# Top-k of a 384-wide score tile by the 128 scores to leave out, with 12 rounds of the 640-wide tile moved ahead of attention

## What is computed

```python
logits = einsum('bthd,bsd->bths', q_idx, k_idx) * IDX_DIM ** -0.5
score = einsum('bth,bths->bts', w_idx, relu(logits))      # w_idx = wi * N_IDX_HEADS ** -0.5
score = where(causal, score, -inf)
_, sel = top_k(score, 256)                                # per query
s = einsum('btkgd,btnkd->btkgn', q, k[sel]) * HEAD_DIM ** -0.5
o = einsum('btkgn,btnkd->btkgd', softmax(s over allowed sel), v[sel])
```

## Time and profile before

| what | value |
|---|---|
| median of 3 runs | 2638.51 us (2636.39 to 2642.58) |
| span of the profiled execution | 2639.8 us |
| mean granted clock of TensorE | 0.963 |
| PE busy over the span | 2413.0 us (91%) |
| DVE busy | 1858.0 us (70%) |
| ACT busy | 1091.3 us (41%) |
| POOL busy | 718.2 us (27%) |

### The profile page before, as it was taken

How to read it: one execution, slowest core, us unless ns; L and a number is a source line. 1 busy time by engine, 2 the same in 40 slices (tenths; PEclk the granted TensorE clock), 3 DMA queues, 4 the chain that set the end, 5 groups by cost and what they waited for, 6 DMA issues and landing times. The chain is left out here.

```text
span 2639.8 us, 35126 instructions
## 1 busy us (share of the span) xinstructions
PE 2413.0 (91%) x13848; PEld 1922.7 (73%) x13848; DVE 1858.0 (70%) x2503; ACT 1091.3 (41%) x1656; POOL 718.2 (27%) x737
## 2 busy tenths in 40 slices
PE   3988968879999999999999899787799999999998
PEld 3966824557777888787877677677687878888887
DVE  6358988984597688887755783676426688777775
ACT  5145379753343334444433442334224334444333
POOL 1332277506545201111223223323263320000000
PEclk8999979989999999999999999899899999999999
DMA  6200154224222643555441110000231344555442
GB/s 230 73 17 24 34 162 113 81 65 152 72 84 92 246 142 123 176 175 176 139 128 41 32 40 17 2 2 2 104 95 41 127 164 171 186 179 177 162 149 80
DMA packets 173849, 282.19 MB, mean 107 GB/s; under 512 B 13407, under 2 KB 86900, under 8 KB 173686
## 3 DMA queue, kind: packets, MB, share of 16 engines
q1 hardware_dynamic: 159184, 255.38, 29.7%
q10 hardware_dynamic: 14502, 24.58, 2.6%
HBM read 252.52 MB, written 27.33 MB: 106 GB/s over the span
## 5 line engine op out<-in xcount | busy, mean ns | idle before, releaser
L1448 ACT ACTIVATE w_hi<-raw 128x1024 fp32r<-128x1024 f32 x198 | 209.0, 1057 | 369.4 <-DVE raw L2123 163.7
L2106 DVE TENSOR_TENSOR w_lo<-raw,w_hi 128x1024 fp32r<-128x1024 f32 x198 | 255.5, 1291 | 126.5 <-ACT w_hi L1448 126.2
L2890 PE MATMUL ps<-w_hi,us_hi 128*128 128x512 f32 x784 | 310.2, 396 | 17.2 <-DVE u_f L2132 10.3
L2890 PE MATMUL ps<-w_lo,us_hi 128*128 128x512 f32 x784 | 309.0, 394 | 0.0
L2890 PE MATMUL ps<-w_hi,us_lo 128*128 128x512 f32 x784 | 308.2, 393 | 0.0
L2578 PE MATMUL ps<-h_hi,w_hi 128*128 128x512 f32 x704 | 286.5, 407 | 8.8 <-issue 4.3
L2580 PE MATMUL ps<-h_hi,w_lo 128*128 128x512 f32 x704 | 276.6, 393 | 0.0
L2579 PE MATMUL ps<-h_lo,w_hi 128*128 128x512 f32 x704 | 276.5, 393 | 0.0
L2156 DVE TENSOR_TENSOR x<-x,ps 128x512 f32<-128x512 f32 x392 | 247.8, 677 | 1.9 <-PE ps L2890 1.6
L2593 PE MATMUL ps<-w_hi,h_hi 128*128 128x512 f32 (+2 forms) x512 | 184.4, 360 | 18.4 <-DVE h_lo L2519 7.2
L1013 POOL TENSOR_TENSOR raw<-raw,gate 128x1024 f32<-128x1024 f32 x32 | 93.3, 2938 | 380.4 <-DMA raw<-in_w_down_dram 380.4
(11 more groups left out here) (472 smaller groups left out, 5323.1 us busy)
## 6 DMA issues: line engine op xcount, KB each, us to landing
h_all<-h_t SPq DMA_DIRECT2D x96, 512.0 KB, 5.6
h_extra<-h_t SPq DMA_DIRECT2D x96, 512.0 KB, 6.5
raw<-in_w_up_dram SPq DMA_DIRECT2D x64, 512.0 KB, 3.9
raw<-in_w_down_dram SPq DMA_DIRECT2D x64, 512.0 KB, 5.8
raw<-in_w_ada_dram SPq DMA_DIRECT2D x48, 512.0 KB, 4.2
raw<-in_w_in_dram SPq DMA_DIRECT2D x32, 512.0 KB, 3.7
raw<-in_w_out_dram SPq DMA_DIRECT2D x32, 512.0 KB, 3.9
h_t<-ht_hi ACTq DMA_DIRECT2D x32, 256.0 KB, 2.2
```

Source lines behind the costliest of these rows:

```text
L1448: s.activation(w_hi[:, slot, :], raw[:, r, :], ACT.Copy).then_inc(sem("w_hi_done"), 1)
L2106: v.tensor_tensor(w_lo[:, slot, :], raw[:, r, :], w_hi[:, slot, :].bitcast(F32), ALU.subtract).then_inc(sem("split_done"), 1)
L2890: last = mm(ps[:, b, :], l[:, c, tok], r, start=(fresh and c == 0 and n == 0), stop=(c == 1 and n == 2), skip_group_check=True)
```

## The change

For tile 2 the kernel now finds the 128 scores to leave out instead of the 256 to keep: 384 - 256 = 128, which is 16 rounds instead of 32. To find the smallest with an operation that finds the largest, the scores are negated (the head weights `wi` of this tile get the opposite sign). They are also stored in reverse order, with `relu` read backwards in `acc_step` and `score[2]` read backwards where the mask is added. Its causal part is written by POOL into `score[2]` itself (a memset and an affine_select with +3.0e38), so the first accumulation adds to `score[2]` and not to `idx0`. The tail of `ROUND` is cut anew: 60 rounds instead of 64 lie ahead of attention. They are 16 of tile 2, 32 of tile 3 and 12 of tile 4. The other 20 rounds of tile 4 are spread over slots 0 to 30.

```diff
-ROUNDS = TOPK // 8
+LEFT_OUT = [t for t in IDX_TILES if (t + 1) * P - TOPK < TOPK]
+def rounds_of(t):
+    return min(TOPK, (t + 1) * P - TOPK) // 8
...
-        ROUND = [(t, r) for t in IDX_TILES for r in range(ROUNDS)]
-        TOPK_Q, TOPK_K, TOPK_LAST = 40, 52, 12
+        ROUND = [(t, r) for t in IDX_TILES for r in range(rounds_of(t))]
+        TOPK_Q, TOPK_K, TOPK_LAST = 40, 52, 8
+        TOPK_AHEAD = [t for t, _ in ROUND[:TOPK_K + TOPK_LAST]].count(4)
...
-                            MICRO += [("topk", ti, r) for r in range(ROUNDS * done // of, ROUNDS * (done + 1) // of)]
+                            left = rounds_of(ti) - TOPK_AHEAD
+                            MICRO += [("topk", ti, TOPK_AHEAD + r) for r in range(left * done // of, left * (done + 1) // of)]
...
                     g.memset(cmask, 0.0).then_inc(sem("pool_step"), 1)
-                    pool.wait_ge(sem("pool_step"), 17 + 2)
+                    for t in LEFT_OUT:
+                        g.memset(score[t], 0.0).then_inc(sem("pool_step"), 1)
+                    pool.wait_ge(sem("pool_step"), 17 + 2 + len(LEFT_OUT))
...
+                    for t in LEFT_OUT:
+                        g.affine_select(out=score[t][:, 0:P], in_=score[t][:, 0:P], compare_op=ALU.is_ge,
+                                        fill=-MASKED, base=1 - P, pattern=[[1, P]],
+                                        channel_multiplier=1).then_inc(sem("idx_ready"), 1)
...
-                v.tensor_scalar(wi[:, t, :], ps[:, t, WI_AT:WI_AT + NH], NH ** -0.5, None,
+                v.tensor_scalar(wi[:, t, :], ps[:, t, WI_AT:WI_AT + NH], -NH ** -0.5 if t in LEFT_OUT else NH ** -0.5, None,
...
-                if r == ROUNDS - 1:
-                    link(v.tensor_scalar(sc, sc, TAKEN, MASKED, ALU.not_equal, ALU.mult))
+                if r == rounds_of(t) - 1:
+                    link(v.tensor_scalar(sc, sc, TAKEN, MASKED, ALU.is_equal if t in LEFT_OUT else ALU.not_equal, ALU.mult))
...
-                v.scalar_tensor_tensor(score[t], relu[:, n % 2, 0:w], wi[:, t, h:h + 1],
-                                       score[t] if h else idx0[:, S - w:S], ALU.mult, ALU.add).then_inc(sem("acc_done"), 1)
+                part = relu[:, n % 2, 0:w]
+                v.scalar_tensor_tensor(score[t], part[:, ::-1] if t in LEFT_OUT else part, wi[:, t, h:h + 1],
+                                       score[t] if h or t in LEFT_OUT else idx0[:, S - w:S], ALU.mult,
+                                       ALU.add).then_inc(sem("acc_done"), 1)
...
-            dve.wait_ge(sem("idx_ready"), 2)
+            dve.wait_ge(sem("idx_ready"), 2 + len(LEFT_OUT))
...
                     bias = cmask[:, 2 * P - w:2 * P] if t < IDX_TILES[0] else score[t]
+                    if t in LEFT_OUT:
+                        bias = bias[:, ::-1]
```

More of the change, by code:

```diff
@@ L638, in build @@
         assert len(SEL_SEQ) == NSEL * (SEL_PASSES - SEL_EARLY)
-        assert TOPK_K + TOPK_LAST == 2 * ROUNDS
+        assert TOPK_K + TOPK_LAST == rounds_of(2) + rounds_of(3) + TOPK_AHEAD
         assert taps_by(NT * NH) == 2 * NCC * QUADS and len(ADA_SLOTS) == N_ADA
@@ L910, in split_qi @@
                                 ALU.subtract).then_inc(sem("qi_split"), 1)
-            nm = [19]
+            nm = [19 + len(LEFT_OUT)]
             def step(ins):
@@ L1870, in sel_step @@
                 if k == 0:
-                    dve.wait_ge(sem("idx_ready"), 2 + NSEL + 2)
+                    dve.wait_ge(sem("idx_ready"), 2 + len(LEFT_OUT) + NSEL + 2)
                     link(v.tensor_tensor(d["acc"], d["sum"], d["wide"], ALU.is_le))
```

## The result

The changed kernel takes 2652.1 us (median, 2644.1 to 2657.8), where the kernel before takes 2640.2 in the same comparison: a ratio of 1.0045, 95% interval 1.003 to 1.006. It is slower by 11.9 us, between 8 and 16. The forecast was slower by 6.7, 2645.2 us, with a range up to 2651. The direction came as forecast and the mechanism in the main; the size did not, and the range ends 1 us short.

The account below looks back on a forecast made before the run. The prediction took PE to bound the projections and POOL and ACT's bisection waits to decide the attention loop. Entry 0.7, stall 4.1, clock 1.9 and loop 0 summed to 6.7 us slower, 2645.2 us, range 2633 to 2651.

Parts of the forecast that it names:

- The bound and the two exits: Projections, 234 to 330 us: bound by PE; the chain from DVE rounds to PE within 0.2 us of the critical path.
- Rounds 8 to 39: DVE ahead of the eighth pass: sixteen rounds at 512, not 384, make PE stand still: +4.1 us, bounds 3.5 and 4.5.
- Clock: PE at tm_in(3), behind the new gap: matmuls run at the low clock, +1.9 us, bounds 0 and 3.4.
- Entry: POOL's memset and affine_select ahead of the split PE waits for at its first index matmul: +0.7 us, bounds 0.5 and 1.2.
- To the loop: From tm_in(3) to the attention loop: nothing absorbs PE's 6.0 us of delay; DVE's extra 1.3 us cost nothing.
- In the loop: Attention loop: DVE has 21.3 us less to do, off the chain, so 0 us gained; bounds no gain and 12.9 us.
- The sum: Whole kernel: 0.7 + 4.1 + 1.9 + 0 = 6.7 us slower, median 2645.2 us.
- Rival A: Attention loop bound by DVE after all: 12.9 us come back, 2632.3 us, faster; chance 0.13.
- B: Part comes back at nearly tied hand-overs (3.6 us) or the clock does not fall (1.9 less): 2640 to 2642; chance 0.25.
- C: Tile 2's reversed operands: backward reads cost double, 4.4 us more, 2649.6 us; chance 0.06.
- D: PE's stall does not come, as DVE gets through 512-wide rounds sooner: +0.7 and little else, 2639; chance 0.06.

Follow-up runs that it names:

- the reordered kernel before: The kernel before with its same 96 rounds in another order, so 16 of rounds 8 to 39 are at 512 candidates, not 384: 2646.7 us, ratio 1.0027.
- the run with the short subtraction: The changed kernel with POOL's subtraction for w_lo done on 32 of the 512 columns of each 128x512 weight block: ratio 1.0039.

## Why the prediction was right and wrong

**The bound and the two exits.** That the projections are bound by PE with DVE close behind, and that the chain DVE rounds, `sel_step`, ACT pass, `pr_q` copies, PE is on the edge of the critical path, held: the reordered kernel before makes the same stall out of nothing but widths. But it had nothing to spare, and not 0.2 us. PE starts 0.72 us after the start of the first copy in the kernel before (279.69 after 278.97), and just so in the stalled one (287.08 after 286.36).

**Rounds 8 to 39.** This is the step that failed. I forecast a stall of 4.1 us with bounds of 3.5 and 4.5; the gap is 6.83. The rounds cost what was said: a step with four rounds takes 6.73 us at 512 (267.8 to 274.5) and took 5.66 at 384, 4.3 us more for sixteen. What was missing are the small operations between them. I had carried them over at 0.16 us each. They took 2.3 us more, since they fell beside POOL's weight splits. The forecast even had the mechanism in hand: the 1.24 us copy showed POOL held up by a DVE sum of two SBUF operands. The Trainium skill, "SBUF — State Buffer", section "Who interferes with whom", has it for both sides. I applied it to the rounds, which have one input, found nothing, and didn't ask it of `sel_acc`, `sel_pick` and `sel_low`, which have two. In the reordered kernel `sel_cand` was hit as well, which has one, so the count of inputs alone doesn't sort the small operations. The rest of the miss is the 0.2 us to spare that weren't there, and 0.3 by which PE came sooner: from its start at 234 us to this wait it took 45.4 us, and 45.7 before. Measured so, 4.3 + 2.3 + 0.3 make the 6.83 to within 0.1. The run with the short subtraction confirms the two larger parts.

**Clock.** Forecast 1.9 with the bounds 0 and 3.4; it cost 2.5, as the slow stretch lasted 5.7 us and not the 4.0 of the earlier trace rows. The longer gap isn't the reason. After a gap of 4.12 us, in the run with the short subtraction, PE ran slow for 5.9 us. After the idle stretch near 234 us, 4.84 or 4.85 us long in all eleven profiles, it ran slow for 3.1 to 4.8. To carry over one such length as a fixed price was a guess, and what sets it was not tried.

**Entry.** 0.7 forecast; PE's wait grew by 0.6, and moving the work away brought it back to 2.06.

**To the loop.** I said that nothing absorbs PE's delay, that DVE's rotary step on `pr_k` would be done at 316.6 and that DVE would wait some 4.6 us ahead of `glu_step(3)`. The rotary step was done at 316.7, and DVE waited 5.4. The first is luck. The copies came 7.4 us later and not 4.2, but the rotary step on `pr_q` took 4.5 us where it had taken 7.5, for in the kernel before two of its operations ran beside POOL's subtraction. The slowest of them there, and the same operation in the changed kernel:

```profile
287.11 2.62 DVE L1836 TENSOR_TENSOR ropet<-pr_q,sinv 128x256 f32<-128x256 f32 x1
```

```profile
293.65 0.42 DVE L1850 TENSOR_TENSOR ropet<-pr_q,sinv 128x256 f32<-128x256 f32 x1
```

So two misses of about 3 us cancelled, both for the most part from POOL's work beside DVE's. What I did not see either is that the slack of DVE was itself made by the stall. It waited 1.1 us for the copies, 2.7 for `k_hi` and 5.4 ahead of `glu_step(3)`, all behind the stall, and 0.5 in all in the kernel before. When the first stall was taken away, the second hand-over took its place. Whether the 1.3 us of rounds that DVE carries more would cost anything under a better cut was not tried.

**In the loop.** 0 us returned, as forecast. The evidence is stronger than the forecast's own: 32 rounds or 20 in it make no difference, and 31 rounds taken out are worth 2 us. It ran 1.2 us longer from `gate_sum` to slot 32 (125.4 after 124.2), and so did every kernel that entered it 8 to 10 us late, with 20 rounds or with 32. What makes it longer was not tried and stays open.

**The sum.** 7.4 at `tm_in(3)`, 2.5 of clock and 1.2 in the loop make 11.1 of the 11.9 us; in the second profile of the changed kernel they are 6.8, 2.6 and 1.5, 10.9. The rest is within the interval. Rival A (the loop bound by DVE) is refuted, B (a part comes back) did not come, C (backward reads cost double) is refuted by 556 beside 553 ns, and D (no stall) likewise. The range was too narrow because both ends of its largest term came from one kind of instruction, the rounds.

## What to carry to other kernels

When a chain is within a fraction of a microsecond of the critical path, price everything in it, the small operations between the large ones too, and ask of each what runs beside it at its new place. Before work is moved from one stage to another, look which engine binds each stage: here DVE was full where the work went and free where it came from. And when a stall goes at one hand-over, look what the engines behind it do with the time: here it came back at the next, until fewer rounds stood ahead.

## What was not expected of the hardware

- A DVE operation on 128x3 elements with both inputs in SBUF took 1.30 us instead of 0.16 beside POOL's 128x512 subtraction, and ended with it. POOL's cast did the same on a smaller scale (0.36). One with a single tensor input took 1.12 us beside the subtraction in the reordered kernel.
- The length of the idle stretch did not tell how long PE then stayed at 1.2 GHz under dense matmuls: 5.7 to 6.1 us after 6.83 (three profiles), 5.9 after 4.12 (one), and 3.1 to 4.8 after 4.84 or 4.85 (eleven).
- Reading a 384-element f32 operand backwards cost DVE nothing measurable: 791 ns beside 798, 556 beside 553.
- Two executions of the same kernel, alike to 0.5 us at 340 us, were 6.5 us apart at 600, with a granted clock of 0.80 in one and 0.90 in the other from 558 to 608 us.
